# One RWKV/attention kernel: the triangular inverse starts three attention units earlier, and the zero products move into its steps

## The chip, the cores and the metric

The kernel runs on one NeuronCore of a Trainium2 chip. Its metric is the device time of one execution in microseconds (us); smaller is better. Five engines work on their own instruction queues and meet in semaphores: TensorE (PE, with its weight loads shown apart as PEld), VectorE (DVE), ScalarE (ACT), GpSimd (POOL) and SyncE (SP), which here issues most DMAs.

## The reference, cut to what matters

Two transformer blocks work on 256 tokens of width 1024. The first block, in which the change lies, mixes two halves of the width: eight heads of RWKV-7 time mixing, and eight heads of a sparse attention in three branches (compressed, selected, window). It then goes through the output projection and the feed-forward part; the second block follows. In outline:

```
p      = rms_norm(x) @ w_in
y_rwkv = rwkv7_time_mix(p[:, :rwkv])     # S = S*w + (S a) b^T + v k^T ; y = S r, token by token
y_nsa  = g0*attn(q, k_cmp, v_cmp) + g1*attn(q, k_sel, v_sel) + g2*attn(q, k_win, v_win)
h      = x + concat(y_rwkv, y_nsa) @ w_out
h      = h + (silu(h_n @ w_gate) * (h_n @ w_up)) @ w_down
```

## The kernel before, in words

The token-by-token recurrence is computed in two chunks of 128 tokens. For each of 8 heads and 2 chunks (16 "RWKV units") that takes the inverse of a lower triangular 128x128 matrix. The inverse is built by doubling. 16x16 blocks are inverted on VectorE (`small_inverse`), travel through DRAM, and come back by eight small DMAs into `Mm` (semaphore `blocks_back`). Three levels (`lv` 4, 5, 6) then join blocks, four units at a time, which makes the twelve entries of `STEPS`. Step q consists of: a product `rwkv_P(q)` on TensorE into bank `ps[0]`; a copy on ScalarE from there to `Pb` (L1529, semaphore `P_ev`); a second product, here called dM(q), into `ps[1]` (semaphore `dM_ps`); and on VectorE the writing of the result into `Mm` or `Mt` (`M_ready`). In the first level it also takes 32x32 transposes of `Mm` to `Mt` (L2217 once at the start, L2238 and L2239 in each step, `Mt_ready`).

Between the parts of the steps stand the attention's units, `nsa(i)`, 34 in number: i below 17 has 128 keys, the rest 256. Number 8 and number 25 are the compressed branch. A unit is a pipeline over three engines. TensorE's `nsa(i)` issues the score product S(i), then the value product o(i-3), then the transposes T(i-2). VectorE's `nsa(i)` adds the bias and takes the maximum for unit i (L2358). ScalarE's `nsa(i)` does the exponential of unit i-1 (L1572) and the copy of the transposed probabilities of unit i-2 out of PSUM (L1580). So S(i) waits until VectorE is through with unit i-2, whose bank it takes, and o(i-3) waits for ScalarE's copy of unit i-3. After the last unit of a branch, VectorE's `nsa(i)` also scales and adds the branch's result (`nsa_result`); that falls on i = 10, 11 and so on.

The order on each engine is written by hand: the code of `rwkv()` on TensorE, ScalarE and VectorE names the same units in the same order. `NSA_FIRST` is the first unit inside the steps, and `NSA_STEPS[q]` says how many units stand in step q: one ahead of dM(q) and the rest behind P(q+1). `stay_busy(n, bank)` issues n products of 128x128 zeros on TensorE, whose results nobody reads. `compress_out` is the second part of the compression, and `A_rest` on VectorE (L2290) reads the banks that the RWKV products before it filled (semaphore `A_read`). TensorE's order around the change is

```
compress_out()
pe.wait_ge(s["A_read"], A_FIRST_READ + 14)
stay_busy(5, 0)
pe.wait_ge(s["A_read"], A_FIRST_READ + RWKV_UNITS)
for i in range(1, NSA_FIRST):
    nsa(i)
    stay_busy(4, 0)
i = NSA_FIRST
rwkv_P(0)
```

Of the kernel before, what the change touches and what calls it, by code (L numbers as in the profile page):

```python
# [95 lines left out]
def build(nc, x_in, wstream, gains, consts_in, masks_in, scratch, tri, inv, out):  # L96
    ctx = ExitStack()
    with ctx:
# [21 lines left out]
        s = {n: ctx.enter_context(nc.semaphore(n)) for n in names}  # L120
# [80 lines left out]
        A_FIRST_PS, A_FIRST_READ = 4, 6  # L201
# [33 lines left out]
        nSS, nPp, nPT = W(8192, 3, T), W(8960, 3, T), W(9728, 2, 2 * P)  # L235
        obr = gb[:, 1, 0:512].rearrange("p (h n) -> p h n", h=8)
        onsa = gb[:, 0, :].rearrange("p (t n) -> p t n", t=TT)
        NSA_FIRST, NSA_STEPS, BRANCHES = 4, [2, 2, 2, 2, 3, 3, 2, 3, 3, 2, 2, 2], (1, 0, 2)
        MOVED = {"out": 16 * QUADS, "in": 16 * QUADS + 16, "inverse out": 16 * QUADS + 32}
        MT_AT, n = {}, 0  # L240
        for q, (lv, k) in enumerate(STEPS):
# [253 lines left out]
        def _(pe):  # L495
# [3 lines left out]
            def mm(o, l, r, start=True, stop=True):  # L499
                return pe.matmul(o, l, r, start=start, stop=stop, skip_group_check=True)  # L500
# [13 lines left out]
            def stay_busy(n, bank):  # L514

                for _ in range(n):
                    mm(ps[bank][:, 0:P], zk[:, 2, :], zk[:, 2, :])
# [329 lines left out]
            def tiles(lv):  # L847
                n = 1 << lv
                if lv == 4:
                    return [(slice(HD * b, HD * (b + 1)),) * 2 for b in range(2)]  # L850
                return [(slice(2 * n * b, 2 * n * b + n), slice(2 * n * b + n, 2 * n * (b + 1))) for b in range(P // (2 * n))]
# [20 lines left out]
            def rwkv():  # L872
                rwkv_A(4)
                rwkv_A(5)
                pe.wait_ge(s["tok_ev"], 4)
                pe.wait_ge(s["cmp_row"], 1)
                compress_T()
                rwkv_A(6)
                nsa(0)
                rwkv_A(7)  # L880
                compress_out()
                pe.wait_ge(s["A_read"], A_FIRST_READ + 14)
                stay_busy(5, 0)
                pe.wait_ge(s["A_read"], A_FIRST_READ + RWKV_UNITS)
                for i in range(1, NSA_FIRST):
                    nsa(i)
                    stay_busy(4, 0)
                i = NSA_FIRST
                rwkv_P(0)
                for q, (lv, k) in enumerate(STEPS):  # L890
                    nsa(i)
                    i += 1
                    pe.wait_ge(s["P_ev"], q + 1)
                    if q:
                        pe.wait_ge(s["M_ready"], q)
                    pe.wait_ge(s["Mt_ready"], MT_AT[5, k - 1] if lv == 5 and k else MT_AT[lv - 1, k])
                    for j in range(4):
                        u, c = 4 * k + j, 64 * j
                        if lv == 6:
                            last = mm(ps[1][0:64, c:c + 64], Pb[64:128, q % 2, c:c + 64], Mt[64:128, u, 64:128])  # L900
                            continue
                        for b, (even, odd) in enumerate(tiles(lv)):
                            f = slice(c + 32 * b, c + 32 * (b + 1))
                            if lv == 4 or b == 0:
                                last = mm(ps[1][odd, f], Mt[odd, u, odd], Pb[odd, q % 2, f])
                            if lv == 5:
                                last = mm(ps[2][even, f], Pb[odd, q % 2, f], Mt[odd, u, odd])
                    last.then_inc(s["dM_ps"], 1)
                    if q + 1 < len(STEPS):
                        rwkv_P(q + 1)  # L910
                    for _ in range(NSA_STEPS[q] - 1):
                        nsa(i)
                        i += 1
                pe.wait_ge(s["M_ready"], len(STEPS))
                for t in range(TT):
                    if t:
                        pe.wait_ge(s["s_ev"], 1)
                        pe.wait_ge(s["y_ev"], 1)

                    for c in range(4):  # L920
                        o = ps[0][:, c * P:(c + 1) * P]
                        if t:
                            mm(o, arT[:, c, 1, 0:P], Sst[:, c, :], True, False)
                        for h in (2 * c, 2 * c + 1):
                            last = mm(o[:, h % 2 * HD:(h % 2 + 1) * HD], AA4[2 * t + h // 4][:, h % 4, 256:384],
                                      vtok[t][:, h * HD:(h + 1) * HD], not t, True)
                    last.then_inc(s["rhs_ps"], 1)
                    nsa(i)
                    i += 1
                    pe.wait_ge(s["rhs_ev"], t + 1)  # L930
                    for h in range(8):
                        last = mm(ps[1][:, h * HD:(h + 1) * HD], Mt[:, 8 * t + h, :], RH[:, h * HD:(h + 1) * HD])
                    last.then_inc(s["sa_ps"], 1)
                    nsa(i)
                    i += 1
                    pe.wait_ge(s["sa_ev"], t + 1)
                    if t:
                        rwkv_T(0)
                        piece(0, 0)
                    if not t:  # L940
                        for c in range(4):
                            o = ps[2][:, c * P:(c + 1) * P]
                            mm(o, bktok[:, 0, c * P:(c + 1) * P], SA[:, c * P:(c + 1) * P], True, False)
                            last = mm(o, bktok[:, 1, c * P:(c + 1) * P], vtok[0][:, c * P:(c + 1) * P], False, True)
                        last.then_inc(s["s_ps"], 1)

                    for c in (2, 3, 0, 1):
                        o = ps[1][:, c * P:(c + 1) * P]
                        if t:
                            mm(o, arT[:, c, 1, P:2 * P], Sst[:, c, :], True, False)  # L950
                        for h in (2 * c, 2 * c + 1):
                            A, oh, hs = AA4[2 * t + h // 4], o[:, h % 2 * HD:(h % 2 + 1) * HD], slice(h * HD, (h + 1) * HD)
                            mm(oh, A[:, h % 4, 128:256], SA[:, hs], not t, False)
                            last = mm(oh, A[:, h % 4, 384:512], vtok[t][:, hs], False, True)
                        if c == 3:
                            last.then_inc(s["y_late"], 1)
                    last.then_inc(s["y_ps"], 1)
                    if not t:
                        nsa(i)
                        i += 1  # L960
# [344 lines left out]
        def _(act):  # L1305
# [212 lines left out]
            def rwkv():  # L1518
                compress_act(0)
                compress_act(1)  # L1520
                act.activation(small[:, 61:62], C("neg_half", 0, 1), ACT.Exp)
                nsa(0)
                compress_out()
                for i in range(1, NSA_FIRST):
                    nsa(i)
                i = NSA_FIRST
                for q in range(len(STEPS)):
                    act.wait_ge(s["P_ps"], q + 1)
                    A(act.copy(Pb[:, q % 2, 0:256], ps[0][:, 0:256]), "P_ev")  # L1529
                    for _ in range(NSA_STEPS[q]):  # L1530
                        nsa(i)
                        i += 1
                for t in range(TT):
                    act.wait_ge(s["rhs_ps"], t + 1)
                    A(act.copy(RH, ps[0][:, :]), "rhs_ev")
                    nsa(i)
                    i += 1
                    if t:
                        w_hi(0, BASE["w_out"], 1)
                    act.wait_ge(s["sa_ps"], t + 1)  # L1540
                    A(act.copy(SA, ps[1][:, :]), "sa_ev")
                    nsa(i)
                    i += 1
                    if t:
                        w_hi(0, BASE["w_out"], 2)
                        act.wait_ge(s["y_late"], 2)
                        piece(0, 0)
                        piece(0, 1)
                    act.wait_ge(s["y_ps"], t + 1)
                    A(act.copy(ytok[:, t, :], ps[1][:, :]), "y_ev")  # L1550
                    if not t:
                        nsa(i)
                        i += 1
                        w_hi(0, BASE["w_out"], 0)
# [427 lines left out]
        def _(v):  # L1982
# [218 lines left out]
            def rwkv():  # L2201
# [5 lines left out]
                nsa(0)  # L2207
                A_rest(14, 16)
                compress()
                for i in range(1, NSA_FIRST):  # L2210
                    nsa(i)
                i = NSA_FIRST
                for q, (lv, k) in enumerate(STEPS):
                    qs, nx = slice(4 * k, 4 * k + 4), slice(4 * k + 4, 4 * k + 8)
                    if (lv, k) == (4, 0):
# [605 lines left out]
```

## Time and profile before

| what | value |
|---|---|
| median of 3 runs | 1398.68 us (1398.54 to 1399.22) |
| the profiled execution: its time | 1398.15 us |
| its span in the profile | 1396.3 us |
| mean granted TensorE clock | 0.995 of full |
| TensorE busy | 1368.1 us, 98% |
| VectorE busy | 943.5 us, 68% |
| ScalarE busy | 689.1 us, 49% |

The span runs from the first to the last instruction of the profiled execution; 1.85 us of that execution's time lie outside it. A share such as "TensorE 98%" is a mean over all stages. The stage of the inverse runs from about 119.6 to 170 us, 50 us of the 1396.3. All times below are counted from the span's start.

### The profile page before, as it was taken

The page shows a single profiled execution, that of the slowest core. Times are in us where ns is not written, and L with a number is a line of the kernel's source. Part 1 is how long each engine was busy: PE and PEld are TensorE (multiplying, and loading weights), DVE is VectorE, ACT ScalarE, POOL GpSimd, SP SyncE. Part 2 cuts the span into 40 slices and gives each one's busy share as a digit, 9 for nine tenths or more (in the row PEclk, how much of TensorE's full clock was granted, in tenths as well). Part 3 has the DMA queues.
Part 4 walks back from the last instruction along what each step waited for, and adds up shares of the span by engine and source line. Part 5 has one row for each costly group of instructions (what it writes and reads, how often), then busy time and mean ns, then how long its engine had stood idle before and what let it go on. Part 6 is the DMA issues. An engine that isn't in the chain of part 4 may idle for free. (4 is left out here: it accounts for less than half of the span.)

```text
span 1396.3 us, 25767 instructions
## 1 busy us (share of the span) xinstructions
PE 1368.1 (98%) x10188; PEld 1261.5 (90%) x10188; DVE 943.5 (68%) x1539; ACT 689.1 (49%) x1107; POOL 82.3 (6%) x137
## 2 busy tenths in 40 slices
PE   8999999999999999999999999999999999999997
PEld 8897788999989999899989999999998988899997
DVE  4778567766668666577577666676665676676665
ACT  6764545433454443376654433444433756643442
POOL 1031010000020000000000000100000123000000
PEclk9999999999999999999999999999999999999999
DMA  9355015655536555433356555365555423465540
GB/s 360 137 170 189 2 34 224 226 180 192 205 106 227 219 181 185 177 116 129 119 210 228 195 180 188 133 232 203 193 180 181 151 92 137 181 226 182 197 162 31
DMA packets 33070, 239.48 MB, mean 172 GB/s; under 512 B 6864, under 2 KB 13280, under 8 KB 14304
## 3 DMA queue, kind: packets, MB, share of 16 engines
q1 hardware_dynamic: 30320, 234.84, 46.4%
q10 hardware_dynamic: 2672, 3.58, 0.8%
q8 instruction: 52, 0.85, 0.2%
q14 instruction: 26, 0.21, 0.0%
HBM read 236.15 MB, written 2.25 MB: 171 GB/s over the span
## 5 line engine op out<-in xcount | busy, mean ns | idle before, releaser
L500 PE MATMUL ps<-uT_h,w_gu 128*128 128x256 f32 x3520 | 600.2, 277 | 2.1 <-ACT uT_h L1335 2.0
L500 PEld LDWEIGHTS ps<-uT_h,w_gu 128*128 128x128 f32 x3520 | 532.7, 188 | 12.8 <-issue 4.7
L500 PE MATMUL ps<-uT_l,w_gu 128*128 128x256 f32 x1760 | 474.6, 277 | 0.0
L500 PEld LDWEIGHTS ps<-uT_l,w_gu 128*128 128x128 f32 x1760 | 325.3, 188 | 0.0
L500 PE MATMUL ps<-w_dn,h_r 128*128 128x512 f32 x1320 | 320.4, 392 | 0.3 <-DVE h_r L2089 0.3
L500 PEld LDWEIGHTS ps<-w_dn,h_r 128*128 128x128 f32 x1320 | 239.7, 188 | 46.7 <-issue 1.5
L1387 ACT CAST w_gu<-ring 128x2048 fp32r<-128x2048 f32 x110 | 209.9, 1908 | 139.5 <-PE ps L500 139.1
L2047 DVE TENSOR_TENSOR w_gu<-ring,w_gu 128x2048 fp32r<-128x2048 f32 x110 | 252.1, 2292 | 35.0 <-ACT w_gu L1387 35.0
L1400 ACT ACTIVATE wk<-wk 128x256 f32<-128x256 f32 x110 | 46.0, 418 | 265.6 <-DVE wk L2078 265.5
L2080 DVE TENSOR_TENSOR us<-ps,bc 128x256 f32<-128x256 f32 x110 | 46.5, 422 | 185.5 <-PE ps L500 185.5
L1393 ACT CAST w_dn<-ring 128x1024 fp32r<-128x1024 f32 x110 | 115.7, 1052 | 76.3 <-PE ps L500 75.7
L2053 DVE TENSOR_TENSOR w_dn<-ring,w_dn 128x1024 fp32r<-128x1024 f32 x110 | 134.1, 1219 | 5.1 <-ACT w_dn L1393 4.9
L500 PE MATMUL ps<-uT_h,ring_r 128*128 128x256 f32 x408 | 113.2, 279 | 0.0
L500 PEld LDWEIGHTS ps<-uT_h,ring_r 128*128 128x128 f32 x408 | 77.0, 189 | 0.6 <-issue 0.2
L500 PE MATMUL ps<-wk 32*32 32x32 f32 (+8 forms) x648 | 70.9, 273 | 2.3 <-DVE small L2358 1.0
L2078 DVE TENSOR_TENSOR wk<-ps,bc 128x256 f32<-128x256 f32 x110 | 46.7, 425 | 34.2 <-PE ps L500 20.9
L500 PE MATMUL ps<-ring_r,uT_h 128*128 128x512 f32 (+2 forms) x176 | 61.7, 351 | 0.0
L500 PEld LDWEIGHTS ps<-wk 128*128 128x128 f32 (+4 forms) x648 | 48.7, 160 | 9.2 <-issue 2.6
L2083 DVE TENSOR_TENSOR wk<-wk,us 128x256 f32<-128x256 f32 x110 | 46.8, 425 | 8.0 <-ACT wk L1400 4.8
L500 PE MATMUL ps<-uT_h,in_h 128*128 128x256 f32 x176 | 49.6, 284 | 1.8 <-DVE ring_r L2040 1.7
L2089 DVE TENSOR_TENSOR h_r<-wk,h_r 128x256 fp32r<-128x256 f32 x110 | 46.8, 426 | 3.8
L500 PE MATMUL ps<-uT_l,in_h 128*128 128x256 f32 x176 | 47.8, 278 | 0.0
(397 smaller groups left out, 1693.3 us busy)
## 6 DMA issues: line engine op xcount, KB each, us to landing
ring<-wstream SPq DMA_DIRECT2D x144, 1536.0 KB, 6.3
cst<-consts_in SPq DMA_DIRECT2D x1, 2185.0 KB, 13.7
wk<-t_row ACTq DMA_DIRECT2D x1, 2048.0 KB, 8.1
wk<-masks_in SPq DMA_DIRECT2D x1, 1216.0 KB, 24.0
x<-x_in SPq DMA_DIRECT2D x2, 512.0 KB, 4.7
ring<-wstream SPq DMA_DIRECT2D x1, 1024.0 KB, 8.8
inh<-gains ACTq DMA_DIRECT2D x2, 512.0 KB, 9.9
tri_blocks<-wk SPq DMA_DIRECT2D x3, 256.0 KB, 2.8
```

The lines of the kernel that those rows point to most:

```text
L500: return pe.matmul(o, l, r, start=start, stop=stop, skip_group_check=True)
L1387: act.copy(w_gu[:, c % 2, 0, :], slot(i)[:, 0:2 * D]).then_inc(s["hi_a"], 1)
L1393: act.copy(w_dn[:, c % 2, 0, :], slot(i)[:, 2 * D:3 * D]).then_inc(s["hi_b"], 1)
L1400: act.activation(sg[:, c % 2, :], sg[:, c % 2, :], ACT.Silu).then_inc(s["silu_ready"], 1)
L2047: v.tensor_tensor(w_gu[:, c % 2, 1, :], slot(i)[:, 0:2 * D], w_gu[:, c % 2, 0, :].bitcast(F32), ALU.subtract).then_inc(s["lo_a"], 1)
L2053: v.tensor_tensor(w_dn[:, c % 2, 1, :], slot(i)[:, 2 * D:3 * D], w_dn[:, c % 2, 0, :].bitcast(F32), ALU.subtract).then_inc(s["lo_b"], 1)
L2078: v.tensor_tensor(h, ps[4 + c % 2][:, 0:T], bc[:], ALU.mult).then_inc(s["gs_ready"], 1)
L2080: v.tensor_tensor(us[:], ps[6 + c % 2][:, 0:T], bc[:], ALU.mult).then_inc(s["us_ready"], 1)
L2083: v.tensor_tensor(h, h, us[:], ALU.mult).then_inc(s["h_mul"], 1)
L2089: v.tensor_tensor(hr[:, 1, :], h, hr[:, 0, :].bitcast(F32), ALU.subtract).then_inc(s["h_ready"], 1)
```

## The change

The first step's product P(0) now stands right behind `compress_out` on TensorE. Units 1, 2 and 3, which stood ahead of it, move into the steps: step 0 has three units instead of two, and so have the steps 9 and 10. At a given place of step 0 the unit's number is lower by three, in the steps 1 to 9 by two, in step 10 by one, and step 11 has the same units as before. The zero products, 17 ahead of P(0) before, become two in each of the eight steps of levels 4 and 5 (16 in all), into bank `ps[1]`, behind the step's first unit and ahead of the wait for `P_ev`.

```diff
-        NSA_FIRST, NSA_STEPS, BRANCHES = 4, [2, 2, 2, 2, 3, 3, 2, 3, 3, 2, 2, 2], (1, 0, 2)
+        NSA_STEPS, BRANCHES = [3, 2, 2, 2, 3, 3, 2, 3, 3, 3, 3, 2], (1, 0, 2)
@@ TensorE, rwkv()
                 compress_out()
-                pe.wait_ge(s["A_read"], A_FIRST_READ + 14)
-                stay_busy(5, 0)
+                pe.wait_ge(s["A_read"], A_FIRST_READ + 13)
+                rwkv_P(0)
                 pe.wait_ge(s["A_read"], A_FIRST_READ + RWKV_UNITS)
-                for i in range(1, NSA_FIRST):
-                    nsa(i)
-                    stay_busy(4, 0)
-                i = NSA_FIRST
-                rwkv_P(0)
+                i = 1
                 for q, (lv, k) in enumerate(STEPS):
                     nsa(i)
                     i += 1
-                    pe.wait_ge(s["P_ev"], q + 1)
                     if q:
                         pe.wait_ge(s["M_ready"], q)
+                    if lv < 6:
+                        stay_busy(2, 1)
+                    pe.wait_ge(s["P_ev"], q + 1)
@@ ScalarE and VectorE, rwkv()
-                for i in range(1, NSA_FIRST):
-                    nsa(i)
-                i = NSA_FIRST
+                i = 1
```

On TensorE, behind the compression's last product (L1059 before, L1057 in the change). Products from `misc` 128x128 are the zero products, those of 64x32 are P and dM, `wk` 128x128 is S of a unit, `misc,wk` is o, and L999 (L997) is T. Before:

```order
L1059 MATMUL ps<-cst,ffb 128x24 x2
L500 MATMUL ps<-misc 128x128 x5
L500 MATMUL ps<-wk 128x128
L500 MATMUL ps<-misc 128x128 x4
L500 MATMUL ps<-wk 128x128
L999 MATMUL ps<-cst,wk 128x128
L500 MATMUL ps<-misc 128x128 x4
L500 MATMUL ps<-wk 128x128
L500 MATMUL ps<-misc,wk 128x64
L999 MATMUL ps<-cst,wk 128x128
L500 MATMUL ps<-misc 128x128 x4
L500 MATMUL ps<-wk 64x32 x8
```

and in the change, at the same place:

```order
L1057 MATMUL ps<-cst,ffb 128x24 x2
L500 MATMUL ps<-wk 64x32 x8
L500 MATMUL ps<-wk 128x128
L500 MATMUL ps<-misc 128x128 x2
L500 MATMUL ps<-wk 64x32 x16
L500 MATMUL ps<-wk 128x128
L997 MATMUL ps<-cst,wk 128x128
L500 MATMUL ps<-wk 128x128
L500 MATMUL ps<-misc,wk 128x64
L997 MATMUL ps<-cst,wk 128x128
L500 MATMUL ps<-wk 128x128
L500 MATMUL ps<-misc,wk 128x64
```

P(0) has moved up past three units and all 17 zero products, and between it and dM(0) (the first eight of the 64x32 x16) now stand one S and two zero products.

On VectorE, around the first transpose of `Mt` (L2217 before, L2211 in the change), the row pair L2358 (L2352) being one unit. Before:

```order
L2404 TENSOR_SCALAR gtok<-gtok,cst 128x8 x2
L2358 ISA wk,small<-ps,cst 128x128
L2358 ISA small 128x1
L2358 ISA wk,small<-ps,cst 128x128
L2358 ISA small 128x1
L2358 ISA wk,small<-ps,cst 128x128
L2358 ISA small 128x1
L2217 STREAM_TRANSPOSE wk<-wk 128x512
L2358 ISA wk,small<-ps,cst 128x128
L2358 ISA small 128x1
L2230 COPY_PREDICATED wk<-msk,ps 128x16x16
```

and in the change:

```order
L2398 TENSOR_SCALAR gtok<-gtok,cst 128x8 x2
L2211 STREAM_TRANSPOSE wk<-wk 128x512
L2352 ISA wk,small<-ps,cst 128x128
L2352 ISA small 128x1
L2224 COPY_PREDICATED wk<-msk,ps 128x16x16
L2232 STREAM_TRANSPOSE wk<-wk 128x512
L2233 STREAM_TRANSPOSE wk<-wk 128x512
L2352 ISA wk,small<-ps,cst 128x128
L2352 ISA small 128x1
L2352 ISA wk,small<-ps,cst 128x128
L2352 ISA small 128x1
```

The transpose comes right behind the compression's last row, and units 2 and 3 now stand behind the two transposes of step 0.

## Rows read from the trace of the kernel before

**Rows 1.** The page: busy times of the engines, granted TensorE clock in 40 slices.

```profile
PE 1368.1 (98%) x10188; PEld 1261.5 (90%) x10188; DVE 943.5 (68%) x1539; ACT 689.1 (49%) x1107; POOL 82.3 (6%) x137
PEclk9999999999999999999999999999999999999999
```

**Rows 2.** Busy time by stretch; behind the engines the granted clock, DMA share, GB/s.

```profile
119.64:124.70 5.06, 5.06 (x47) 4.94 (x45) 3.58 (x12) 2.30 (x11) 0.00 (x0) 1.00 0.89 367
...
137.41:140.92 3.51, 2.19 (x50) 1.54 (x49) 3.23 (x11) 1.12 (x6) 0.00 (x0) 0.96 0.00 0
140.92:147.65 6.73, 6.73 (x62) 5.59 (x63) 3.06 (x14) 3.85 (x17) 0.00 (x0) 0.51 0.02 4
147.65:169.87 22.22, 22.08 (x238) 17.54 (x237) 14.65 (x49) 13.37 (x46) 0.00 (x0) 1.00 0.01 2
...
185.20:188.54 3.34, 2.56 (x22) 2.34 (x21) 1.46 (x3) 2.54 (x5) 2.39 (x2) 0.98 0.00 0
188.54:192.00 3.46, 3.46 (x18) 3.46 (x18) 3.29 (x7) 0.47 (x1) 0.00 (x0) 0.52 0.00 0
```

**Rows 3.** Waits of TensorE's weight loads, 119.64 to 149: total, times, longest.

```profile
PEld ps L500 <- ACT wk L1580: 2.7, 9, 0.4
PEld ps L500 <- DVE small L2358: 1.1, 1, 1.1
PEld ps L500 <- issue: 0.7, 3, 0.3
PEld ps L999 <- ACT wk L1572: 0.2, 1, 0.2
```

**Rows 4.** TensorE in order of time: start, duration, operation.

```profile
119.64 1.38 PE L500 MATMUL ps<-misc 128*128 128x128 f32 x10
...
121.08 1.06 PE L500 MATMUL ps<-misc 128*128 128x128 f32 x8
121.97 0.39 PE L500 MATMUL ps<-wk 128*128 128x128 f32 x2
...
124.70 1.07 PE L500 MATMUL ps<-wk 64*64 64x32 f32 x18
...
128.65 0.66 PE L500 MATMUL ps<-wk 64*64 64x32 f32 x16
...
129.70 0.49 PE L500 MATMUL ps<-wk 128*128 128x128 f32 x2
...
130.31 0.98 PE L500 MATMUL ps<-kcT,wk 128*128 128x32 f32 x8
...
144.51 0.80 PE L500 MATMUL ps<-wk 128*128 128x128 f32 x2
```

**Rows 5.** VectorE in order of time.

```profile
121.33 0.50 DVE L2404 TENSOR_SCALAR gtok<-gtok,cst 128x8 f32<-128x8 f32 x2
...
124.05 0.71 DVE L2217 STREAM_TRANSPOSE wk<-wk 128x512 f32<-128x512 f32 x1
...
126.76 0.43 DVE L2230 COPY_PREDICATED wk<-msk,ps 128x256 f32<-128x256 uint8 x1 [0.56 <-PE ps L500]
127.22 0.71 DVE L2238 STREAM_TRANSPOSE wk<-wk 128x512 f32<-128x512 f32 x1
127.97 0.71 DVE L2239 STREAM_TRANSPOSE wk<-wk 128x512 f32<-128x512 f32 x1
128.72 0.29 DVE L2358 CUSTOM_DVE_ANT_0 wk<-ps,cst 128x128 f32<-128x128 f32 x1
```

**Rows 6.** ScalarE in order of time: exponential, its sum, copy, next exponential.

```profile
122.20 0.40 ACT L1572 ACTIVATE wk<-wk,small 128x128 f32<-128x128 f32 x1 [1.56 <-DVE small L2358]
...
122.60 0.24 ACT L1580 COPY wk<-ps 128x128 f32<-128x128 f32 x1
122.84 0.40 ACT L1572 ACTIVATE wk<-wk,small 128x128 f32<-128x128 f32 x1
```

**Rows 7.** The DMAs that bring the small inverses back: issues, and time to landing.

```profile
L465 SPq DMA_DIRECT2D wk<-inv_blocks x8: 328/448/454, 114.0 to 117.3; - x8
...
DMA to landing us min/median/max: 1.7/2.2/2.4
```

More of the change, by code:

```diff
@@ L2209, in rwkv @@
                 compress()
-                for i in range(1, NSA_FIRST):
-                    nsa(i)
-                i = NSA_FIRST
+                i = 1
                 for q, (lv, k) in enumerate(STEPS):
```

## The prediction

> **What bounds the kernel now.** I read the page first. TensorE is busy for 98% of the span and the next engine, VectorE, for 68%; at the resolution of 40 slices the clock never shows below nine tenths [rows 1]. So the whole is bound by TensorE's stream, and a change that neither adds nor removes more than one small product can only pay where TensorE waits or runs slow. The second view, busy time by stretch, shows where that is. From 119.64 to 124.70 TensorE has no idle time, but it does zero products. From 137.41 to 140.92 it is busy for 2.19 of 3.51 us while VectorE is busy for 3.23: there VectorE is the bound for a moment, since the results of the first two branches (units 10 and 11) and the end of level 4 fall together. Right behind it, from 140.92 to 147.65, the granted clock is 0.51, so TensorE is on its lower level, 1.2 instead of 2.4 GHz. The same pair stands once more at the stage's end: 2.56 busy of 3.34 us, then 3.46 us at 0.52. Between them, 147.65 to 169.87, the clock is full [rows 2]. Third, the waits. TensorE's matmul rows hide short ones, so I take those of its weight loads: 4.7 us in the 29.4 us from 119.64 to 149, 2.9 of them for ScalarE (L1580 and L1572), 1.1 for VectorE, 0.7 for no named releaser [rows 3].
>
> The Trainium skill ("Trainium Kernel Development and Optimization", Performance Expectations) calls matmul busy time a bad metric, because matmuls are pipelined, and prefers the weight loads. The trace agrees: matmul rows alone would leave about 1.3 us idle in 137.41 to 140.92 and nothing in the five us before 124.70, the weight loads show 4.7 us. By the first the change could win back 1.3 us of waiting at most, by the second up to 4.7.
>
> **The change part by part.** *Zero products.* One is two instructions; eight instructions take from 121.08 to 121.97, 0.89 us, so one product costs 0.22 us [rows 4]. 17 fall away and 16 come back: -0.2 us of work. The three units' work only moves.
>
> *What the first steps now wait for.* P(0) needs the small inverses. The last of eight DMAs is issued at 117.3 and lands 2.2 us later, at 119.5; P(0) can start where the zeros start now, at 119.64 [rows 4, 7]. It costs me nothing up to a delay of 1.7 us, as the following shows. P(0) is 16 instructions, about 0.55 us, so up to 120.2. Then S(1) and two zeros, up to 120.95. dM(0) needs the transpose of `Mt`. VectorE is through with the compression at 121.33 + 0.50 = 121.83 and the transpose takes 0.71: 122.57 [rows 5]. So TensorE waits from 120.95 to 122.6, **1.65 us**, for VectorE, where before it ran zeros.
>
> *Prices for the walk.* P+dM of level 4: 1.05 us (128.65 to 129.70). A unit of 128 keys on TensorE: 0.6 us (129.70 to 130.31) [rows 4], of which S takes 0.22. On VectorE a step of level 4 takes 126.76 to 128.72, 1.96 us, a unit 0.33 to 0.37 [rows 5]. On ScalarE one unit takes 0.64 us (122.20 to 122.84) [rows 6]. From a product's end to VectorE's start I use 0.2 to 0.3 us.
>
> *Walk.* dM(0) runs 122.6 to 123.2 and P(1) to 123.7. VectorE does step 0 from 123.4 to 125.35, and only then the units 2 and 3, up to 126.05, because they now stand behind the transposes. TensorE does S(2), T(0), S(3), o(0), T(1) by 124.9; S(4) needs VectorE's unit 2, at 125.7: wait **0.85**. o(1) needs ScalarE's exponential of unit 2 (from 125.75) and its copy, done 126.5: wait **0.55**. Then zeros, and dM(1) at 127.3, against 128.65 before. From step 1 on one unit stands ahead of dM as before and the period is again that of VectorE and the copies: dM(2) at 130.2, dM(3) at 133.4, dM(4) at 136.35, dM(5) at 140.75, with waits of 0.2 to 0.4 for the copy of ScalarE once or twice a step, **2.35** in all. The results that made the backlog at 137 to 141 fall into step 4 instead of 3; there TensorE has the wide product of the compressed unit, one unit and two zeros to do beside them, so I find no wait of a microsecond. Waits sum to 5.4 us, against 4.7 before [rows 3]: the walk moves the waiting to the front, it doesn't remove it.
>
> *Sum.* By 143.3 in the walk, TensorE has done step 5 and the units up to S(15). Before, S(16) begins at 144.51, after the same work [rows 4]. Four zero products (0.9 us) are still to come: 144.2, a gain of 0.3. What is left of the low clock before, 144.51 to 147.65, is 3.1 us; about 0.7 of it would be waiting or is bound by the copies, half of the remaining 2.4 us is what the clock costs: gain 1.2. In the 256-key part one pair of units more stands without a step between: -0.2, an estimate from the 0.3 us waits above. That makes **-1.3 us**, if the clock stays full.
>
> *Does it?* The two falls in the trace come behind stretches in which TensorE stood for around 1 us among small products [rows 2]. The first steps now have 1.65 + 0.85 + 0.55 us of waiting in seven, among 64x32 products, and the dense zeros that filled this place are gone. I think it likelier than not that the clock falls here. If it does for as long as the shorter fall (3.4 us), about 2.0 us of work (three units, two pairs of zeros) takes twice as long, of which the 1.4 us of waiting takes up most: +0.6. Bounds: 0 if it doesn't fall; +2.5 if it lasts 6.8 us as the longer one, since 5 us of work then double and 2.5 of waiting absorb the half. The Trainium skill ("TensorE: Matmul & The Clock Gate", Part 1) says that the lower clock is the resting state and that activity releases it. That speaks against thinning the work ahead of level 4, and the trace agrees in that both falls follow thin stretches; it has no thin stretch at 120 to 124 to try it on. With that rule the sum is -0.7, without it -1.3.
>
> *The rest.* The 256-key part, 147.65 to 169.87, has TensorE busy for 22.08 of 22.22 us and ends as before. I let the second fall at 188.54 stand as it is; the kernels before and after issue the same there. SP's queue and POOL's aren't touched; the weight loads that SP issues at 117.8 and after do not wait for anything that moves.
>
> Likeliest: 1398.15 - 0.7 = 1397.45 for an execution like the profiled one, which lies 0.53 us under the median of the runs; so **1398.0 us** for the median.
>
> **The rivals.** *A, forecast:* the wait moves from 140 to 121 and 125, gain under 2.8 us. *B, full clock all the way:* the zeros inside the steps keep the clock up, the steps' waits are filled, and the shift takes away the second fall too, whose 3.4 us cost up to 1.7. Then -1.3 - 1.7 = -3.0, so 1395.7. For it: the zeros now stand where the thin stretch at 137 was. Against it: nothing changes in the stretch 185.20 to 188.54. Stronger, if also half of the waits behind copies went (1.2 us of 2.35): 1394.5. *C, slower:* the thin start brings the clock down for 6.8 us, and the shifted backlog at step 4 still brings it down a second time. Its price: -1.3 + 2.5 + the 1.8 us that the present fall costs, +3.0, so 1401.7. It decides against the change where the early fall costs over 1.3 us, which needs it to last more than about 5 us; to pass 0.2% it needs both. For it: VectorE's step of 1.96 us stands ahead of units 2 and 3, and a slow TensorE feeds it late. Against it: in the walk the waits behind 127.3 stay under 0.4 us, and zeros stand between. *D, nothing changes:* TensorE's instructions are the same but one, and the steps are set by the loop over ScalarE and VectorE; whatever starts earlier waits later. 0 to -0.2, 1398.5.
>
> **How the numbers follow.** A 0.48, D 0.14, B 0.24, C 0.14. About 0.2% (2.8 us) is what a measurement of this kernel can tell from no change. A and D lie within it, B mostly beyond on the fast side, C mostly on the slow side: faster 0.24, same 0.63, slower 0.13. The range, 1395.3 to 1400.6, takes in B's first form and C up to an early fall of 6.8 us without the second one (-1.3 + 2.5, and 0.9 for the walk's own error) and leaves B's strong form and C's full price out.
>
> **What the profile will show.** P(0) at about 119.7 behind the 24x24 products. TensorE idle for 1.2 to 1.9 us until dM(0) at 122.6, released by VectorE's transpose (wrong if `blocks_back` comes later, then P(0) is late and DMA is named). A second wait for VectorE around 125 to 126.5. dM(1) between 127 and 128.5. No idle time over 0.6 us for TensorE between 136 and 142, and full clock there. A stretch at half clock that begins between 122 and 127. The first product behind the inverse, now at 169.9, between 167.5 and 170.5. What would make me wrong: a clock that stays full in spite of the waits, which moves all to B; or an order on VectorE or ScalarE that adds a wait which I priced at 0.3 us in each of the eight zero-filled steps.

## The result, and the profile after

| | median | lowest to highest | executions |
|---|---|---|---|
| before | 1402.19 us | 1398.54 to 1404.66 | 14 |
| the change | 1407.48 us | 1400.85 to 1412.09 | 14 |

The change is slower: ratio 1.0038, 95% interval 1.0023 to 1.0053, some 5 us. The profiled execution took 1407.42 us, its span is 1405.5 us, 9.2 more than before. Each execution also gives its mean granted TensorE clock. Four of the 14 have 0.994 to 0.996 and took 1400.85 to 1401.82 us; ten have 0.988 to 0.990 and took 1406.3 to 1412.09 us. The profile is of the second kind. That is why the two profiles lie 9.3 us apart and the medians only 5: the ten have a mean of 1408.7 us, the four one of 1401.5, and the 14 executions of the kernel before one of 1401.5.

The page of the changed kernel, answering to [rows 1]:

```profile
PE 1376.4 (98%) x10186; PEld 1267.4 (90%) x10186; DVE 943.6 (67%) x1539; ACT 689.3 (49%) x1107; POOL 82.1 (6%) x137
PEclk9997899999999999999999999999999999999999
```

VectorE and ScalarE have done the same work in the same busy time as before. TensorE has two instructions fewer (one zero product) and 8.3 us more busy time, and the clock dips in the fourth and fifth slice, 105 to 176 us. The same kernel by stretch, columns as in [rows 2]:

```profile
119.47:122.55 3.08, 1.59 (x25) 1.31 (x23) 2.86 (x7) 1.27 (x6) 0.00 (x0) 1.00 0.87 347
122.55:150.41 27.86, 27.83 (x247) 24.10 (x248) 14.64 (x46) 9.13 (x37) 0.00 (x0) 0.51 0.43 182
150.41:171.00 20.59, 20.18 (x253) 16.30 (x253) 11.26 (x44) 11.82 (x45) 0.00 (x0) 1.00 0.01 2
```

A mean clock of 0.51 over 27.86 us, where the levels are 1 and 0.5, makes 2 x (1 - 0.51) x 27.86 = 27.3 us at 1.2 GHz. Before it was 6.8 us in this stage [rows 2]. The sequence on TensorE, start, duration and operation:

```profile
119.24 0.30 PE L1057 MATMUL ps<-cst,ffb 24*128 24x24 f32 x2
119.47 1.15 PE L500 MATMUL ps<-wk 64*64 64x32 f32 x18
120.45 0.61 PE L500 MATMUL ps<-misc 128*128 128x128 f32 x4
122.55 2.62 PE L500 MATMUL ps<-wk 64*64 64x32 f32 x34 [1.49 <-DVE wk L2211]
...
127.69 1.06 PE L500 MATMUL ps<-misc 128*128 128x128 f32 x4
128.69 1.07 PE L500 MATMUL ps<-wk 64*64 64x32 f32 x16
...
179.20 2.38 PE L500 MATMUL ps<-wk 128*128 128x64 f32 x18
```

P(0) starts at 119.47, dM(0) at 122.55 behind a wait of 1.49 us for the transpose (L2211), and from about 122.6 on everything takes up to twice as long: the 34 instructions with dM(0) and P(1) 2.62 us where the same count took 1.54 before, two zero products 1.06 us up to their end where they took 0.61 in step 0. The first product behind the inverse (128x64 x18) starts at 179.20; before, at 169.87, from a compression that ended 0.2 us later. I use the distance from the 24x24 products to this one as the **length of the stage**: 50.46 us before (119.41, where its 24x24 products stand, to 169.87), 59.96 after. The waits of the weight loads from 119.4 to 151.5 in the changed kernel:

```profile
PEld ps L500 <- issue: 3.2, 6, 1.6
PEld ps L500 <- ACT wk L1576: 1.3, 6, 0.2
PEld ps L997 <- issue: 0.5, 1, 0.5
```

5.0 us, about as many as before [rows 3], with the copies' share halved: at half rate TensorE is the bound and hardly waits for ScalarE. So neither more work nor more waiting explains 9.5 us. The clock does. What is low is the rate, not the busy time: from 122.55 to 150.41 TensorE is busy for 27.83 of 27.86 us.

The second fall of the kernel before, 188.5 to 192 [rows 2], isn't there in the changed kernel, though the instructions around it are the same and wait as long for VectorE (0.78 us in both):

```profile
197.87:201.30 3.43, 3.43 (x32) 3.43 (x32) 3.26 (x7) 0.62 (x2) 0.00 (x0) 1.00 0.00 0
```

From the stage's end to the first feed-forward product the kernel before takes 51.53 us (169.87 to 221.40) and the change 51.25 (179.20 to 230.45). So that fall of 3.4 us had cost about 0.3 us. At that product the change is 9.05 us behind, of the 9.2 by which the span grew.

### The profile page after: what moved, and what is told of

Same layout as the page of the kernel before. It is cut to its first block and busy times, and to the rows that moved or that the text cites. A ratio compares the mean times of both kernels' runs of the same rounds, so it can differ in the third digit from the quotient of the medians.

```text
span 1405.5 us, 25765 instructions
## 1 busy us (share of the span) xinstructions
PE 1376.4 (98%) x10186; PEld 1267.4 (90%) x10186; DVE 943.6 (67%) x1539; ACT 689.3 (49%) x1107; POOL 82.1 (6%) x137
## 5 line engine op out<-in xcount | busy, mean ns | idle before, releaser
L500 PE MATMUL ps<-wk 32*32 32x32 f32 (+8 forms) x648 | 74.8, 288 | 2.9 <-DVE wk L2211 1.5
L500 PEld LDWEIGHTS ps<-wk 128*128 128x128 f32 (+4 forms) x648 | 52.7, 177 | 10.1 <-issue 4.7
```

## The experiments

All are built on one of the two kernels, and each computes the full reference; zero products compute nothing that is read. "Low" is the time at 1.2 GHz in the stretch 123 to 150 of the profile, 54 us x (1 - mean clock); the mean clock has two digits, so low is good to 0.3 us. A ratio is taken against executions of the kernel before that ran beside the kernel in question. Their medians go from 1398.75 to 1402.36 us, so kernels of different rows are compared by their ratios and stages and not by their medians.

| kernel | ratio to before | executions by mean clock | profile: low | stage |
|---|---|---|---|---|
| before | 1 | | 7.0 | 50.46 |
| change | 1.0038 (1.0023 to 1.0053) | 4 of 14 at 0.994 or more | 27.0 | 59.96 |
| 1. ten zeros in step 0 | 0.9990 (0.9974 to 1.0007) | 12 of 12 at 0.995 or more | 0 | 50.48 |
| 2. old order, new zeros | 1.0029 (1.0015 to 1.0043) | 0 of 12 | 26.5 | 59.74 |
| 3. new order, 17 zeros in step 0 | 1.0030 (1.0013 to 1.0046) | 2 of 12 | 17.3 | 55.57 |
| 4. no zeros | 1.0020 (1.0005 to 1.0035) | 0 of 12 | 23.8 | 55.08 |
| 5. early transpose | 1.0040 (1.0024 to 1.0056) | 0 of 6 | 17.3 | 56.32 |
| 6. six zeros in step 0 | 1.0024 (1.0002 to 1.0045) | 6 of 12 | 0 | 50.24 |
| 7. early transpose, six zeros | 1.0012 (0.9993 to 1.0031) | 7 of 12 | 20.5 | 57.72 |
| 8. before, nine zeros more | 0.9996 (0.9983 to 1.0010) | 12 of 12 | 3.2 | 50.80 |
| 9. six zeros in steps 1 to 7 | 1.0048 (1.0033 to 1.0063) | 4 of 4 | 7.0 | 57.91 |
| 10. small zeros in step 0 | 1.0007 (0.9989 to 1.0025) | 8 of 11 | 23.8 | 59.3 |

The profile is one execution; for 6, 7 and 10 the other kind of execution exists beside it, and for the change and 3 a rarer one.

**1. Ten zero products in step 0.** It asks whether the clock or the new order costs the time.

```diff
                     if lv < 6:
-                        stay_busy(2, 1)
+                        stay_busy(2 if q else 10, 1)
```

> The changed kernel with ten zero products instead of two in step 0, in the place where TensorE waited 1.5 us for the transpose; the steps 1 to 7 keep two each. Theory 1 (the granted clock falls because the stretch behind the compression has become thin, and it then stays low for eight steps because these stay thin at half rate): the clock stays full from 119 to 137, the stage ends 8 to 10 us earlier than in the changed kernel's profile (first product behind the inverse at 168 to 171 instead of 179.2), time 1397 to 1399 us, mean clock 0.995 or more. Rival (the new order on VectorE and ScalarE is what costs, whatever the clock): time stays above 1403 us.

Median 1398.83 us. TensorE in order of time, and the stretch 123 to 150:

```profile
119.21 0.30 PE L1057 MATMUL ps<-cst,ffb 24*128 24x24 f32 x2
...
120.42 2.40 PE L500 MATMUL ps<-misc 128*128 128x128 f32 x20
122.75 1.54 PE L500 MATMUL ps<-wk 64*64 64x32 f32 x34
...
127.44 0.65 PE L500 MATMUL ps<-wk 64*64 64x32 f32 x16
...
136.95 1.04 PE L500 MATMUL ps<-wk 32*32 32x32 f32 x42
...
169.69 2.38 PE L500 MATMUL ps<-wk 128*128 128x64 f32 x18
```

```profile
123.00:150.00 27.00, 25.16 (x402) 21.02 (x400) 19.18 (x64) 13.57 (x59) 0.00 (x0) 1.00 0.43 179
```

Eight products that compute nothing take 9.5 us off the stage (59.96 to 50.48). The order is the change's. So the cost is the clock's, not the order's. (One of the twelve, 1406.12 us at 0.995, lies outside the range I gave; it has no profile.) But at a full clock the stage is also no shorter than before, 50.48 against 50.46.

**2. The old order with the new place of the zeros.** The other half alone.

```diff
-                stay_busy(5, 0)
...
                 for i in range(1, NSA_FIRST):
                     nsa(i)
-                    stay_busy(4, 0)
...
-                    pe.wait_ge(s["P_ev"], q + 1)
                     if q:
                         pe.wait_ge(s["M_ready"], q)
+                    if lv < 6:
+                        stay_busy(2, 1)
+                    pe.wait_ge(s["P_ev"], q + 1)
```

> The kernel before with its old order of units (1, 2 and 3 ahead of the first product of the inverse), but with the zero products of the change: none ahead, two in each of the steps 0 to 7. It takes apart the order and the place of the zeros. Theory 1: the stretch from 119.6 is thin here too (three units without zeros between), so the clock falls in part of the executions; where it falls, about 1405 us, where it doesn't, about 1398. Rival (the new order alone is the cost): 1397 to 1399 us in all executions and a clock of 0.995.

Median 1406.91 us. TensorE in order of time:

```profile
118.87 0.30 PE L1059 MATMUL ps<-cst,ffb 24*128 24x24 f32 x2
119.85 0.68 PE L500 MATMUL ps<-wk 128*128 128x128 f32 x4 [0.69 <-DVE uT L2290]
120.90 0.30 PE L999 MATMUL ps<-cst,wk 128*128 128x128 f32 x1 [0.36 <-DVE inh L2399]
121.68 0.49 PE L500 MATMUL ps<-wk 128*128 128x128 f32 x2 [0.48 <-DVE small L2358]
```

Without the zeros between them, the units 1 to 3 wait for VectorE too, 1.5 us in three pieces, and the clock falls, in all twelve executions and not in a part of them as I had expected. The old order with it is as slow as the change. So this part of the edit is enough for the cost, without the moved units.

**3. The new order with 17 zeros in step 0, none later.** `stay_busy(17, 1)` if q is 0.

> The changed kernel's order of units, with 17 zero products in step 0 and none in the later steps: as many as before, and about where they stood. Theory 1: no early fall; 17 products take 3.8 us of which 1.7 fill the wait, so step 0 ends some 2 us later than the walk says; one shorter fall around 137 to 150 as in the kernel before. Time 1397 to 1401 us. Rival (order alone): above 1403 us with a full clock at 120 to 137.

Median 1404.27 us; a miss. The clock passes the start and falls at about 128.5, in step 1, for 17.3 us:

```profile
123.00:150.00 27.00, 25.76 (x295) 21.18 (x293) 16.62 (x55) 10.78 (x46) 0.00 (x0) 0.68 0.40 171
```

I had expected the fall where it was before, behind 137. But in the new order there is a thin place between P(1) and dM(1) (waits of 0.52 us for VectorE's unit 2 and 0.19 us for the copy), and the zeros behind it are gone here. Kernel 1 has the same two waits at 125 to 126.5, with two zeros behind them, and keeps its clock. So with the new order both places need something dense. The rival's time (above 1403 us) came true, but not its condition, a full clock from 120 to 137.

**4. No zero products.** `stay_busy(2, 1)` is deleted.

> The changed kernel without any zero product. Theory 1: the early fall comes as in the changed kernel, in all executions, and since the small products of the steps are all that is left, the clock stays low at least as long, 27 us or more. Each pair of zeros saved is worth 0.44 us at half rate, so the 16 save 3 us at most against the changed kernel: 1404 to 1410 us. Rival (the zeros in the steps are themselves the cost, since they stand in a chain that waits): faster than the changed kernel by more than 4 us.

Median 1403.39 us, just under the range I gave, and the low stretch, 23.8 us, is shorter than the 27 or more that I had expected. By the ratios this kernel and the change can't be told apart (the intervals overlap); in the profiles the stage is 4.9 us shorter (55.08 against 59.96). The rival's mark, more than 4 us faster than the change, is met by the raw medians (4.1 us) and by the stage. 16 zeros at 0.44 us each, the price at half rate, are 7.0 us. So up to half of the change's 9.5 us may be put down to the zeros themselves, which don't bring the clock back; how much of the 4.9 is the 3 us of low clock less isn't separated.

**5. The wait ahead of dM(0) taken away, the thinness left.** On VectorE the first transpose goes ahead of `compress()`.

```diff
                 A_rest(14, 16)
+                v.wait_ge(s["blocks_back"], 16 * 8)
+                V(v.transpose(Mt[:, 0:4, :], Mm[:, 0:4, :]), "Mt_ready")
                 compress()
...
-                    if (lv, k) == (4, 0):
-                        v.wait_ge(s["blocks_back"], 16 * 8)
-                        V(v.transpose(Mt[:, qs, :], Mm[:, qs, :]), "Mt_ready")
```

> The changed kernel with the first transpose of Mt on VectorE ahead of the compression's last rows (it waits for the small inverses there), so that dM(0) no longer waits 1.5 us for it; zero products as in the change, two in step 0. It takes the wait away and leaves the stretch thin. Theory 1 (thinness, not the wait, brings the clock down): dM(0) starts at about 121.0 instead of 122.55, yet the clock falls as before in most executions; 1404 to 1408 us. Rival (the one wait of 1.5 us is what tips the clock): clock full in nearly all executions, time 1396 to 1399 us.

Median 1405.37 us. TensorE:

```profile
120.33 1.15 PE L500 MATMUL ps<-wk 64*64 64x32 f32 x18
121.32 0.61 PE L500 MATMUL ps<-misc 128*128 128x128 f32 x4
121.86 1.54 PE L500 MATMUL ps<-wk 64*64 64x32 f32 x34
...
125.95 0.49 PE L500 MATMUL ps<-wk 128*128 128x128 f32 x2 [1.06 <-DVE small L2351]
```

No wait is left between the zeros and dM(0), and the small products run at full rate. But the edit didn't take the waiting away: TensorE now waits for VectorE's unit 2, 1.06 us ahead of S(4), where kernel 1 waits 0.52. The clock falls at 127.4, in the zeros and the small products behind that wait, for 17 us. So the wait in front of dM(0) isn't needed for a fall; whether a fall needs a wait of about a microsecond, this kernel doesn't show.

**6 and 7. Six zero products in step 0,** without and with the early transpose (`stay_busy(2 if q else 6, 1)`).

> The changed kernel with six zero products in step 0 instead of two (ten kept the clock up). Six take 1.3 us and end before the transpose, so they cost nothing on TensorE: at full clock the stage must end with that of two zeros or better. Theory 1 with a gradual threshold: the clock stays up in some executions and falls in others; median between 1398 and 1405 us, clocks of 0.989 and 0.998 side by side. If six suffice: 1397 to 1399 us.

> Early transpose and six zero products in step 0 together: dM(0) at about 121.9, some 0.8 us ahead of the kernel with ten. Theory 1: where the clock stays full, 1396.5 to 1398.5 us, a few tenths under the kernel before; if VectorE's step is the bound (its chain starts 0.8 us earlier) the whole 0.8 us is kept at the end of level 4 and given back in the 256-key part, where TensorE is the bound and the work is the same.

Both are divided. In 6, six executions have a clock of 0.998 or 0.999 and five of them took 1398.79 to 1399.47; six have 0.989 to 0.991 and took 1404.9 to 1411.26. The means of the two sixes are 8.8 us apart with the same instructions, which shows the price of the clock without any edit. In 7 seven of twelve have 0.995 or more. The stage of the full-clock profile of 6 is 50.24 us, 0.2 better than before. The early transpose brought nothing that the spread lets me see: of its executions at a high clock two lie in the 1396.5 to 1398.5 us that I gave, five took 1401.69 us or more.

**8. The kernel before with three zeros more in each of the steps 3 to 5.**

> The kernel before with its 17 zero products where they are, and three more in each of the steps 3, 4 and 5, ahead of dM, around the stretch where its own clock fell at 140.8. Theory 1 (a thin stretch brings the clock down): no fall there, mean clock 0.998, and the low stretch of 6.8 us gives back up to 1.8 us against nine zeros of 0.22 us, of which the wait of 1.1 us hides half: 1397 to 1399 us, at most 1 us from the kernel before. Rival (the fall at 140.8 cost several us): 1395 to 1396.5 us.

Median 1399.16 us, ratio 0.9996. I had expected no fall; one still comes, at 143.5, and lasts 3.2 instead of 6.8 us. The stage is 50.80 us, 0.3 longer than before. The nine zeros and the shorter fall are in this number together, and the run can't tell them apart.

**9. Six zeros in the steps 1 to 7, two in step 0.** It asks what holds the clock down.

> The changed kernel with two zero products in step 0 as in the change, but six instead of two in each of the steps 1 to 7. The early fall must come as before, since step 0 is the same. It asks what holds the clock down for 27 us once it has fallen. Theory 1 (the steps stay thin at half rate): with six dense products in each step it comes back within 3.4 to 10 us, and the profile shows a low stretch of at most 14 us; the 28 zeros more cost 6 us at full clock, part of it in waits, so the time is 1403 to 1408 us. Rival (once down, it stays down until the inverse's small products are over, whatever stands between): low for 24 us or more, each zero at 0.44 us, 1412 us or more.

Median 1405.21 us.

```profile
123.00:150.00 27.00, 26.27 (x343) 23.38 (x344) 16.57 (x55) 10.45 (x45) 0.00 (x0) 0.87 0.45 188
```

The clock falls at 124.2, 1.1 us behind the start of dM(0) (in the change 0.1 us behind it), and is back after 7.0 us instead of 27. All four executions have a mean clock of 0.996 or 0.997, against 0.990 or less in ten of the change's 14. So the low clock isn't bound to the inverse: how long it stays hangs on what stands in the steps that follow. "Thin" here means made of small products, since in the change TensorE is busy all through its low stretch. The 28 zeros eat most of what they bring: the low stretch is 20 us shorter, the stage 2.05 us (57.91 against 59.96), and the ratio is not below the change's.

**10. Small zero products in the wait.** Behind the two large ones, step 0 gets 44 products of 32x32 zeros.

```diff
+                    if not q:
+                        for _ in range(22):
+                            for r in (slice(0, 32), slice(32, 64)):
+                                mm(ps[1][r, 0:32], zk[r, 2, 0:32], zk[r, 2, 0:32])
```

> The changed kernel with 44 further products of 32x32 zeros in step 0 behind its two large ones, which fill the 1.5 us wait for the transpose with small products in the form of the inverse's own. Theory 1 in its sharp form (small products don't keep the clock up, large ones do): the weight loads and products show a busy stretch from 120 to 122.5, yet the clock falls in most executions as in the change, 1404 to 1409 us. Rival (any product counts, it's the idle time that brings the clock down): clock full as with ten large zeros, 1397 to 1400 us.

Median 1398.61 us; my sharp form is refuted. Eight of eleven executions keep 0.997 or more, against none above 0.996 in the change. Three fall, the profiled one among them:

```profile
118.90 1.14 PE L500 MATMUL ps<-wk 64*64 64x32 f32 x18
119.88 2.12 PE L500 MATMUL ps<-misc 128*128 128x128 f32 x92
121.97 1.54 PE L500 MATMUL ps<-wk 64*64 64x32 f32 x34
...
125.04 0.75 PE L500 MATMUL ps<-wk 128*128 128x128 f32 x2 [0.52 <-DVE small L2356]
```

There TensorE has a product in flight from 118.9 to 124.5, waits 0.52 us for VectorE's unit 2, and the clock falls at 125.1. The profiles of 1 and 6 have a wait as long at the same place (0.52 and 0.53 us) and no fall. Small products help; whether less surely than ten large ones, three falls of eleven against none to 0.991 or less in the twelve of kernel 1 don't settle.

## Why the prediction was wrong

**Right.** That 98% busy leaves only waits and the clock. (One reading there compares unlike stretches: the matmul rows' own idle time in 119.64 to 149 is 1.84 us, not 1.3, beside the weight loads' 4.7.) P(0) at 119.7 (119.47), not late for its DMAs; the wait for the transpose, 1.65 us (1.49), dM(0) at 122.6 (122.55). The walk is the clearest success, read against the full-clock kernel 1: dM(1) at 127.3 (127.44), dM(4) at 136.35 (136.95). Its waits for VectorE's unit 2 and for the copies, 0.85 and 2.9 us, were 0.7 and 3.4 by the weight loads there. The fall itself, "begins between 122 and 127", came at about 122.6, and the mechanism was rival C's first half.

**The step that failed: how long the fall lasts and what it costs.** The text let it last "as long as the shorter fall (3.4 us)", priced +0.6, with 6.8 us and +2.5 as the far bound. It lasted 27.3 us and cost 9.5. The price of a low microsecond was about right (2.5/6.8 = 0.37 us forecast, 9.5/27.3 = 0.35 measured); the length was not. Both bounds were taken from the falls of the kernel before, as if length belonged to the chip. Experiment 9 shows that it hangs on what follows: with dense products there it was 7.0 us. Before, the first fall ended at 147.65, where the 256-key units begin, and the second at 192, in products of 128x128 and 128x64; that this is why they were short is argued, not shown. At step 0 eight steps of small products followed. I had also counted the zeros in the steps as what would keep the clock up; they don't lift it once it is low (27.3 us with them, 23.8 in experiment 4 without) and cost double then, though they may hold it while it is high (1 against 3). Rival C's 3.0 us needed a second fall at step 4; one long one did it.

**The second fall** at 188.54 was left standing in the sum because nothing changes there. It is gone in the profiles of the change and of 1, 3, 4, 5, 7, 8 and 9, and there in those of 2, 6 and 10, which have the same instructions around it. Rival B priced it at up to 1.7 us; by the distance behind the stage it costs 0.3 (51.53 to 51.60 us with it, 51.21 to 51.27 without).

**The term -1.3 us was 0.** At full clock the stage has the length of before (50.48, with six zeros 50.24, against 50.46). The walk up to step 5 held. What it took for "the rest of the low clock before", 1.2 us, is too much: kernel 1 reaches dM(7) with P(8) at 147.95 with two 256-key units of 1.34 us still to do, so 150.6, where before it starts at 150.98. Counted from the 24x24 products, which come 0.2 us earlier in kernel 1, that is a gain of 0.15 us, and the part behind dM(7) takes it back (priced at 0.2). Since the stage at a full clock is no shorter than with a fall of 6.8 us, the low clock of before seems to have been mostly hidden in waits; this compares two orders, and no run has the old order at a full clock.

**The Trainium skill's rule** ("TensorE: Matmul & The Clock Gate", Part 1: the low clock is the resting state, activity releases it) was weighed as speaking against the change and given +0.6. The runs agree with it more than I did: in experiments 2 and 4, clocks of 0.993 and less in all 24 executions. But having a product in flight wasn't the activity that releases the clock here: in the change TensorE is busy for all of the 27 us at half rate.

**Luck and spread.** The forecast was counted from three executions of the kernel before, 1398.68 us; fourteen gave 1402.19. So of the 9.5 us between 1398.0 and 1407.48, 3.5 belong to the spread of the kernel before and not to the change. The upper end of the range is also 0.2 us low by its own sum: 1398.68 - 1.3 + 2.5 + 0.9 is 1400.8, not 1400.6. Neither touches the sum: it forecast -0.7 us, and the change cost 5.

**Open.** What exactly a stretch must hold to keep the clock isn't settled. The wait in front of dM(0) isn't needed for a fall (5), a wait of 0.52 us goes with both a fall and none (10, 1), and the same kernel goes both ways (6, 7, 10). No kernel here keeps the stretch free of waits and thin, so waiting and thinness aren't parted. Nor whether the four better executions of the change fell late or for a short time; only their mean clock, 0.994 to 0.996, is known.

## What to carry to other kernels

Zero products that fill a wait ahead of a chain of small products are part of the kernel: before moving them, ask what TensorE does in the few us behind the place they leave, and how long the part behind it stays thin: the falls here lasted 17 to 27 us with thin steps behind them and 7 with dense ones. Price a low clock by the work that follows, not by the length of the falls that the profile happens to show; and where the engine waits anyway, a fall can be nearly free (0.3 us for 3.4). And where a kernel is this near to a fall, one profile is one throw: list the mean clock of every execution before trusting a difference of 5 us.

## What the runs showed of the hardware

Apart from the clock there is a second spread of some 4 us in all these kernels, the one before too (29 executions beside the kernels 5 to 8: 1396.43 to 1404.87 at clocks of 0.994 to 0.998). The profile of kernel 1, 1401.67 us with a full clock, is such an execution. Its stage isn't longer; the time lies in the second block. From the block's first products to the start of a later feed-forward pass the kernel before takes 306.5 us (591.15 to 897.61), kernel 1 310.9 (590.65 to 901.51). Products of one kind, 780 to 800 us, kernel 1:

```profile
L500 PE MATMUL ps<-uT_h,w_gu 128*128 128x256 f32 x83 | 14.9, 281 | 0.0
L500 PE MATMUL ps<-uT_l,w_gu 128*128 128x256 f32 x42 | 11.8, 281 | 0.0
```

and before, same stretch:

```profile
L500 PE MATMUL ps<-uT_h,w_gu 128*128 128x256 f32 x80 | 13.8, 277 | 0.0
L500 PE MATMUL ps<-uT_l,w_gu 128*128 128x256 f32 x41 | 11.3, 276 | 0.0
```

No idle time, a granted clock of 1.00 in both, and each product 4 to 5 ns longer. What slows it no view here shows. It may be why the executions of the change with a low clock come in two groups, near 1407.5 and 1411.5 us (only one of them has a profile), and it is as large as the effect that was to be measured.
